# Modulation vectors of one diffusion step: weight blocks stationary and two conditioning columns moving, and the cached keys turned earlier

## The reference, cut to what matters

```python
def _modulation(cond, w_mod, b_mod):
    m = jax.nn.silu(cond) @ w_mod + b_mod        # (1024) @ (1024 x 6144)
    return jnp.split(m[:, None, :], N_MOD, axis=-1)

shift1, scale1, gate1, shift2, scale2, gate2 = mod
h = _rmsnorm(x, norm1_g) * (1 + scale1) + shift1
u = h @ w_in                                     # (1280 tokens x 1024) @ (1024 x 5376)
```

## Time and profile before

| | |
|---|---|
| median of 3 runs | 1966.56 us (1965.03 to 1967.02) |
| time of the profiled execution | 1965.78 us |
| span of its trace | 1963.7 us |
| TensorE matmul busy | 1916.6 us (98%) |
| VectorE, ScalarE, GpSimd busy | 1177.3, 752.0, 522.5 us |
| mean granted TensorE clock | 0.994 |

### The profile page before, as it was taken

One profiled execution on the slowest core, in us unless ns is written; L12 is line 12 of the kernel. 1 busy time (PEld: TensorE's weight loads), 2 busy tenths in 40 slices (PEclk: granted clock), 3 DMA queues, 4 the chain that ended last, 5 costly groups with the idle time before them and its releaser, 6 DMA issues.

```text
span 1963.7 us, 27547 instructions
## 1 busy us (share of the span) xinstructions
PE 1916.6 (98%) x10488; PEld 1690.0 (86%) x10488; DVE 1177.3 (60%) x2098; ACT 752.0 (38%) x1380; POOL 522.5 (27%) x403
## 2 busy tenths in 40 slices
PE   8899999999989999999999999999999999999999
PEld 3799989989988899978888888888888888888899
DVE  5699795266656666437514865555443335799862
ACT  3512232455545555444422332222222223454453
POOL 0000000544443443224451234444444441000000
PEclk9999999999999999999999999999999999999999
DMA  7461334634424442356551132222222224867663
GB/s 306 178 198 49 110 120 173 158 91 99 100 75 102 103 104 63 123 185 203 156 193 68 56 98 94 82 91 81 70 70 70 70 70 162 272 214 231 199 196 137
DMA packets 226146, 256.33 MB, mean 131 GB/s; under 512 B 37856, under 2 KB 170720, under 8 KB 224992
## 3 DMA queue, kind: packets, MB, share of 16 engines
q1 hardware_dynamic: 226016, 254.58, 41.9%
HBM read 193.98 MB, written 60.56 MB: 130 GB/s over the span
## 4 chain that ended last, share of the span: by engine, by line
PE 82%; DVE 7%; DMA 5%; ACT 3%; issue 2%; POOL 1%; SPq 1%; DVEq 0%; ACTq 0%; POOLq 0%
PE ps_all L144 58%; PE ps_all L2143 4%; PE ps_all L2144 4%; PE ps_all L2145 4%; PE ps_all L1051 2%; PE ps_all L1028 2%; PE ps_all L1037 2%; DMA w_raw<-w_in_dram 2%; DMA wmod_then_mixers<-w_mod_dram 1%; PE ps_all L2177 1%; DMA branch_and_gates<-branch_dram 1%; PE ps_all L445 1%; DVE X L2610 1%; DVE X L2604 1%; DVE AL L2614 1%
## 5 line engine op out<-in xcount | busy, mean ns | idle before, releaser
L144 PE MATMUL ps_all<-AH,w_hi 128*128 128x448 f32 (+3 forms) x1408 | 509.4, 362 | 7.9 <-DVE wmod_then_mixers L653 3.3
L144 PE MATMUL ps_all<-AH,w_lo 128*128 128x448 f32 (+3 forms) x1408 | 497.9, 354 | 0.0
L144 PE MATMUL ps_all<-AL,w_hi 128*128 128x448 f32 (+3 forms) x1408 | 497.9, 354 | 0.0
L144 PEld LDWEIGHTS ps_all<-AH,w_hi 128*128 128x128 f32 x1408 | 267.4, 190 | 30.3 <-DVE wmod_then_mixers L653 3.6
L144 PEld LDWEIGHTS ps_all<-AH,w_lo 128*128 128x128 f32 x1408 | 266.8, 190 | 21.4
L144 PEld LDWEIGHTS ps_all<-AL,w_hi 128*128 128x128 f32 x1408 | 267.9, 190 | 18.9
L2678 DVE TENSOR_TENSOR quarter<-ps_all,quarter 128x512 f32<-128x512 f32 x140 | 96.5, 689 | 175.7 <-PE ps_all L144 173.6
L2532 POOL TENSOR_TENSOR slot_lo<-w_pair,slot_hi 128x512 fp32r<-128x512 f32 x96 | 130.4, 1383 | 174.9 <-ACT slot_hi L2340 174.9
L1233 POOL TENSOR_TENSOR w_lo<-w_raw,w_hi 128x1024 fp32r<-128x1024 f32 x21 | 50.3, 2394 | 361.7 <-ACT w_hi L1074 361.7
L1196 DVE TENSOR_TENSOR PT<-ps_all,PT 128x512 fp32r<-128x512 f32 (+2 forms) x144 | 76.3, 567 | 93.6 <-ACT PT L1113 93.6
L144 PE MATMUL ps_all<-AH,slot_hi 128*128 128x256 f32 (+1 forms) x384 | 129.6, 338 | 1.1 <-DVE hidden L2649 1.1
(11 more groups left out here) (256 smaller groups left out, 4118.7 us busy)
## 6 DMA issues: line engine op xcount, KB each, us to landing
w_raw<-w_in_dram SPq DMA_DIRECT2D x42, 512.0 KB
wmod_then_mixers<-w_mod_dram SPq DMA_DIRECT2D x20, 1024.0 KB, 7.9
w_pair<-w_gu_dram SPq DMA_DIRECT2D x20, 1024.0 KB, 5.3
hidden_in<-hidden SPq DMA_DIRECT2D x77, 256.0 KB, 3.2
hidden<-quarter SPq DMA_DIRECT2D x50, 256.0 KB, 2.1
branch_and_gates<-gates SPq DMA_DIRECT2D x16, 768.0 KB, 4.5
w_down_rows<-w_down_dram SPq DMA_DIRECT2D x44, 256.0 KB, 3.9
gates<-gate_rows SPq DMA_DIRECT2D x42, 224.0 KB, 2.2
```

Source lines behind the costliest of these rows:

```text
L144: mm = nc.tensor.matmul(out, w, a[:, k, cols[0]:cols[1]], start=(first and part == 0), stop=(last and part == 2))
```

## The change

- `early_modulation(k)` makes 16 matmuls instead of 4: a 128x128 block of the weights is stationary, the two columns of `silu(c)` for block `k` move, and the result, 128 x 2, is added to its two columns of `mod_cols`, which now lies in bank 7 and has 32 columns. All 128 matmuls are one accumulation, opened by one matmul of a zeroed tile (`kt_ctx[:, 0, :]`) with 32 columns of the identity.
- `turn_modulation` and the two copies before it (L580, L748) go. `mod_bias` reads bank 7 as soon as all 8 blocks are used.
- `load_mod(0)` and `load_mod(1)` wait for `w_used` in place of `mod_turned`.
- `turn_cached_k` moves from between units 1 and 2 to before unit 0; its wait for the load of `cached_k` moves with it.
- VectorE clears `kt_ctx[:, 0, :]` as its first instruction.

```diff
-        rows = g.ps_all[0:2, 4:8, :].rearrange("p b n -> p (b n)")
-        mod_cols = g.ps_all[:, 3, 0:4 * KD]
+        mod_cols = g.ps_all[:, 7, 0:4 * KD]
...
                 else:
-                    sp.wait_ge(mod_turned, 1)
+                    sp.wait_ge(w_used, KD)
...
             def early_modulation(k):
                 pe.wait_ge(w_in[k % 4], 16 * (k // 4 + 1))
-                for q in range(4):
-                    mm = nc.tensor.matmul(rows[:, q * 512:(q + 1) * 512], g.cs[:, 2 * k:2 * k + 2], w_early[:, k % 4, q * 512:(q + 1) * 512],
-                                          start=(k == 0), stop=(k == KD - 1))
+                if k == 0:
+                    pe.wait_ge(ones_ready, 1)
+                    nc.tensor.matmul(mod_cols, kt_ctx[:, 0, :], g.ident[:, 0:4 * KD], start=True, stop=False)
+                for m in range(2 * KD):
+                    mm = nc.tensor.matmul(mod_cols[:, 2 * m:2 * m + 2], w_early[:, k % 4, m * P:(m + 1) * P], g.cs[:, 2 * k:2 * k + 2],
+                                          start=False, stop=(k == KD - 1 and m == 2 * KD - 1))
                 mm.then_inc(w_used, 1)
...
-            def turn_modulation():
-                pe.wait_ge(xn_ready, KD)
-                pe.wait_ge(rows_out, 2)
-                for m in range(2 * KD):
-                    mm = nc.tensor.transpose(mod_cols[:, 2 * m:2 * m + 2], mod_rows[0:2, m * P:(m + 1) * P], g.ident[0:2, 0:2])
-                mm.then_inc(mod_turned, 1)
...
-            turn_modulation()
+            turn_cached_k()
...
             for u in range(2, MIX):
-                if u == 2:
-                    turn_cached_k()
...
-            act.wait_ge(w_used, KD)
-            nc.scalar.activation(mod_rows[0:2, 0:D], rows[:, 0:D], ACT.Copy).then_inc(rows_out, 1)
...
+            nc.vector.memset(kt_ctx[:, 0, :], 0.0)
             nc.vector.memset(g.ones[:, :], 1.0)
...
             dve.wait_ge(w_used, KD)
-            nc.vector.tensor_copy(mod_rows[0:2, D:2 * D], rows[:, D:2 * D]).then_inc(rows_out, 1)
-            dve.wait_ge(mod_turned, 1)
             mod_bias(g, 0, 2, mod_cols, mod1)
```

More of the change, by code:

```diff
@@ L181, in front_engines @@
         w_early = early[:, 0:4 * 2 * D].rearrange("p (b n) -> p b n", b=4)
-        mod_rows = early[:, 0:2 * D]
         w_mod_sb = early[:, 0:2 * 2 * D].rearrange("p (b n) -> p b n", b=2)
@@ L199, in front_engines @@
         sq_done, root_ready, rstd_ready, diag_ready, rb_done = sem("x_squared"), sem("x_root"), sem("x_rstd"), sem("diag_ready"), sem("rb_done")
-        xn_ready, w_used, rows_out, mod_turned, mod1 = sem("xn_ready"), sem("wmod_used"), sem("mod_rows_out"), sem("mod_turned"), sem("mod1_step")
+        xn_ready, w_used, mod1 = sem("xn_ready"), sem("wmod_used"), sem("mod1_step")
         act_scaled, t_ready, ah_ready, al_ready, spilled = sem("act_scaled"), sem("t_ready"), sem("ah_ready"), sem("al_ready"), sem("spilled")
```

## The result

The changed kernel takes 1989.89 us (median of 4 runs, 1985.05 to 1998.23) against 1966.79: ratio 1.0114, 95% interval 1.0093 to 1.0136, slower by about 1.1%. Forecast were 1984.0 and a range of 1973 to 1996. The profiled execution is the fastest of the four: 1985.05 us, span 1982.9, against 1965.78 and 1963.7 before, so 19.3 us more. The forecast sum for the profiled execution was 18.2.

The account below looks back on a forecast made before the run. TensorE, busy 1916.6 of 1963.7 us, was taken as the bound, the start of `mod_bias` passing straight through. +19.1 (later `mod_bias`) - 0.9 (moved keys) = +18.2, added to the profiled 1965.78, gave 1984.0; range 1973 to 1996.

Parts of the forecast that it names:

- A thin record costs 0.111 us at the full clock and 0.213 at half: Modulation matmuls with 2 moving columns: a block of 32 records takes 3.57 us at full clock, 6.83 at half.
- The clock falls in thin runs though TensorE is busy: Modulation blocks: full clock lasts 2.9 us (2.2 and 3.6 in two earlier stretches); rival of no fall, 1964.5 us, chance 0.09.
- Transposes lift it again, with about one failure of four: Turned rows between blocks restore full clock; each failure costs 2.6 us; chance 0.73; rival of never lifting, 1994 us, 0.10.
- the four blocks: Modulation blocks 0 to 3 on TensorE: 4.2 us each, 16.8 together, plus 2.6 for one at half clock throughout.
- the groups: Three groups of 16 turned rows between the first four modulation blocks, begun at half clock: 3.3 us each, 9.9 together.
- the spread: TensorE's spread of 1/rms before block 4, 20 records: 16 in 3.3 us, 4 at 0.111, together 3.75 us.
- blocks 4 to 7: Last modulation blocks, 128 records: 26 at full clock (2.9 us), 102 at 0.213 (21.7), together 24.6 us.
- Copies and turns go: After block 7, copies (1.21 us) and turns (1.11) vanish; `mod_bias` starts 0.05 later, at 69.95 against 50.88: +19.1.
- keys cost nothing before unit 0 and save 0.9 behind unit 1: Eight cached-key turns leave the chain at 89.17 (-0.87 us), hiding before unit 0's first product; load lands 63.2, before 69.9.
- GpSimd's clears cost nothing: The clears wait for `w_used` as before and are needed only after 24 pairs, so 0 us.
- The pairs pass every us of `mod_bias` on: At unit 0 the 24 modulated pairs set the pace, so each us of `mod_bias` is a us of the kernel.
- a slow stretch not met: 24 products at 83.17 take 6.00 us in place of 4.45; its loss or gain was counted as scatter, 1.5 either way.

Follow-up runs that it names:

- The mix of thin and wide: Changed kernel with three 512-column matmuls added to each modulation block, after its 5th, 10th and 15th two-column matmul, results unread: 2016.82 us, ratio 1.025 to the kernel before.
- the wide-then-thin run: Changed kernel with blocks 0 to 3 as 512-column matmuls, results dropped, only blocks 4 to 7 in the new form: 1978.3 against 1970.26 us, ratio 1.0047.
- second profile: The changed kernel, unaltered, profiled once more: 1980.26 us for one run.
- thin alone: Changed kernel with the turning of the cached keys put back between units 1 and 2: 1987.88 against 1968.55 us for the kernel before, ratio 1.0097.
- the by-quarter version: Kernel before, modulation rows copied and turned by quarter, GpSimd's clears late, keys turned between third chunks of units 0 and 1: 1965.65 against 1968.55 us, 0.9983; again 0.998.

## Why the prediction was right

Its steps, each against the profile after:

- *A thin record costs 0.111 us at the full clock and 0.213 at half.* Measured 0.112 and 0.213. The two moving columns and the common bank add nothing.
- *The clock falls in thin runs though TensorE is busy.* Right, in every profile of the form. The mix of thin and wide showed both paces in one program, and the wide-then-thin run showed the fall out of a full clock. (One of the two stretches that the forecast leaned on was misread: by its own row, the last wide matmul before L2031 starts at 1093.58 and takes 0.39, so the full clock lasted 3.4 us behind it and not 3.6. The sum does not hang on that.)
- *Transposes lift it again, with about one failure of four.* They do lift it, and whether they do is the scatter; the number was too low. In the five profiles whose first four blocks are those of the changed kernel, 8 of 20 groups failed: none in two of them, two in the profile after, three in the run with the clears held back and three in the one with blocks 4 to 7 shortened. No failures give `mod_bias` at 64.9 and 65.3, two give 71.9, three give 75.1, so each costs about 3.3 us; the sum had 2.6, from 67.3 without any. So the forecast of 69.9 with one failure stands near the 71.9 with two because the start without failures was put about 2 us too high.
- *Term by term to the end of block 7* (69.9 forecast, 71.87 measured): the four blocks took 18.3 with one at half clock throughout (19.4 forecast), the groups 9.8 (9.9), the spread 4.5 (3.75), blocks 4 to 7 27.1 (24.6). The last two are the term that was mis-sized. The sum gave the end of the spread and a first part of blocks 4 to 7 the full clock; here the spread did not lift it, so all of them ran at half. Where it did lift it they took 24.5 (second profile) and 24.4 (thin alone).
- *Copies and turns go, keys cost nothing before unit 0 and save 0.9 behind unit 1.* Right; the keys' load landed 9 us before it was wanted (issued at 57.7, 5.1 to land).
- *GpSimd's clears cost nothing.* Wrong. In the kernel before, the clear of 128x2624 had run beside VectorE's copy out of PSUM (48.37); with the copy gone it falls on the first modulated piece, and puts unit 0 off by 1.6 us in the profiled execution. The prediction moved the clears in time and did not ask what stood beside them then.
- *The pairs pass every us of `mod_bias` on.* Right: +21.0 at `mod_bias`, with the 1.6 the +22.6 at unit 0, of which 0.9 and a slow stretch not met (1.7) came off by unit 2.

So the mechanism was right, and the close number is in part luck. 18.2 forecast and 19.3 measured are nearly the same by errors that cancel in part: +2.0 (up to `mod_bias`), +1.6 (the clears), -1.7 (the stretch) and about -1 later. The median lies 4.8 higher than the profiled run, since that was the fastest of four, and the slowest, 1998.23, lies above the forecast range. The other three have no trace; by the scatter of the profiled ones they had more failures, which is argued and not shown. Their mean granted clocks, 0.975, 0.978 and 0.975 against 0.978 of the profiled one, fit that in two cases and say nothing in the third (1988.06).

## What to carry to other kernels

To swap the operands of a small f32 matmul so that the weights are stationary saved nothing here, even though it did away with copies and turns. A record with a load of 128x128 weights took 0.11 us at full clock with 1, 2 or 128 moving columns, so a block took as long as in the other form (3.6 us), and with so few moving columns the clock fell to half. A TensorE row that reads "busy" must be read together with the granted clock. And where an edit removes an instruction at a hand-over, look at what all the other engines released by the same semaphore will now run beside.

## What the runs showed that was not expected

VectorE's f32 `TENSOR_SCALAR` from SBUF to SBUF (128x448) waits while GpSimd clears 128x2624: 2.12 to 2.55 us in place of 0.51. VectorE's copy out of PSUM was not held by the same clear: beside it 1024 elements took 1.21 us, while the by-quarter version's copies of 512, with no clear beside them, took 0.68 each. The Trainium skill states it (SBUF — State Buffer, "Who interferes with whom"): a `tensor_scalar` of VectorE can take the pair of ports that it shares with GpSimd, and the one that comes second is blocked wholly. The runs agree as to the waiting: in the changed kernel the piece starts 0.4 us behind the clear and ends 0.24 after it (74.45 to 74.21). With the clears put on the piece the two start within 0.02 us, the piece first (51.33 to 51.35), and it still ends 0.24 after the clear (53.88 to 53.64); which of them came second there, their records do not tell.

The clock seems to have a memory. The mix of ten thin records and one wide matmul kept the full clock for up to 7.6 us at a time (over 30 us with groups of transposes in between) and, once at half, stayed there for 35 us. So whether a stretch keeps its clock seems to depend also on the clock with which it begins; one profile shows this, and whether the mix alone would have held the full clock for longer, had the 12 thin records not stood together, was not tried. A kernel at this edge scatters: 4 runs of the changed kernel spread over 13 us.
